# Seven identity matmuls ahead of the gate and up projections of the 31st expert in a two-layer decoder trunk

## The reference, cut to what matters

```python
def hier_moe(h, wg, bg, we, be, w1, w3, w2):
    ...
    def expert_block(args):
        xi, e = args
        hid = jax.nn.silu(xi @ w1[e]) * (xi @ w3[e])
        return hid @ w2[e]
    ...
for l in range(DEPTH):
    ...
    x = x + g1[:, None, :] * y
    h = rms_norm(x) * (1.0 + sc2[:, None, :]) + sh2[:, None, :]
    x = x + g2[:, None, :] * hier_moe(h, ...)
```

## Time and profile before

| | |
|---|---|
| time, median of 3 runs (lowest to highest) | 1340.63 us (1339.63 to 1341.82) |
| span of the profiled execution | 1345.7 us |
| own time of the profiled execution outside its span | none is recorded |
| PE (matmul) busy | 1260.7 us, 94% |
| DMA bytes, mean rate over the span | 493.50 MB, 367 GB/s |
| DMA rate in the slices in which only experts run | 423 to 431 GB/s |
| mean granted clock of TensorE | 0.975 |

### The profile page before, as it was taken

How to read it: one execution, slowest core, us unless ns; L and a number is a source line. 1 busy time by engine, 2 the same in 40 slices (tenths; PEclk the granted TensorE clock), 3 DMA queues, 4 the chain that set the end, 5 groups by cost and what they waited for, 6 DMA issues and landing times.

```text
span 1345.7 us, 15042 instructions
## 1 busy us (share of the span) xinstructions
PE 1260.7 (94%) x6115; PEld 601.4 (45%) x6115; DVE 414.6 (31%) x938; ACT 235.0 (17%) x499; POOL 109.3 (8%) x139
## 2 busy tenths in 40 slices
PE   6999998999999999989898999999999999889988
PEld 3444476433433333434345457743443343333334
DVE  3574864412121121112114983431212211121112
ACT  2223332311111011101110033231101110010101
POOL 2020003000300300210000010000000000000000
PEclk9999999999999999999899998999999999998989
DMA  9992883799999999999999782569999999999993
GB/s 366 407 291 105 329 345 140 289 414 429 428 428 426 429 428 428 429 427 428 428 423 410 284 317 104 211 259 410 431 427 428 427 428 427 428 428 428 428 428 152
DMA packets 51914, 493.50 MB, mean 367 GB/s; under 512 B 4784, under 2 KB 6072, under 8 KB 20992
## 3 DMA queue, kind: packets, MB, share of 16 engines
q1 hardware_dynamic: 49104, 488.85, 87.8%
q10 hardware_dynamic: 1584, 2.69, 0.5%
q0 software_dynamic: 1152, 0.91, 0.5%
HBM read 489.28 MB, written 3.16 MB: 366 GB/s over the span
## 4 chain that ended last, share of the span: by engine, by line
PE 68%; DMA 23%; DVE 5%; issue 1%; ACT 1%; SPq 0%; DVEq 0%; ACTq 0%; PEldq 0%
PE B L872 26%; DMA ring<-in_moe_w 17%; PE B L889 11%; PE A L899 6%; PE A L788 4%; PE B L692 4%; DMA both<-in_moe_w 2%; PE B L705 2%; PE B L635 2%; DMA ring<-in_ada_w 2%; DMA ring<-in_od_w_in 2%; PE A L852 2%; PE B L599 2%; DVE work L1540 1%; PE B L588 1%
## 5 line engine op out<-in xcount | busy, mean ns | idle before, releaser
L872 PE MATMUL B<-ring,work 128*64 128x512 f32 x1488 | 450.2, 616 | 27.2 <-DMA ring<-in_moe_w 19.0
L1534 DVE TENSOR_TENSOR work<-work,B 64x512 f32<-64x512 f32 x64 | 68.3, 1067 | 627.1 <-ACT work L1949 627.1
L872 PEld LDWEIGHTS B<-ring,work 128*64 128x64 f32 x1488 | 140.2, 141 | 230.6 <-issue 230.0
L889 PE MATMUL B<-ring,work 128*64 128x512 f32 x704 | 159.3, 594 | 0.6 <-ACT work L1953 0.6
L1949 ACT ACTIVATE work<-B 64x512 f32<-64x512 f32 x64 | 37.7, 590 | 581.0 <-PE B L872 580.9
L872 PE MATMUL B<-both,work 128*64 128x512 f32 x272 | 124.7, 613 | 5.8 <-DMA ring<-in_moe_w 5.8
L899 PE MATMUL A<-work 128*128 128x256 f32 x512 | 118.1, 384 | 9.3 <-DVE work L1540 9.3
L899 PEld LDWEIGHTS A<-work 128*128 128x128 f32 x512 | 94.6, 190 | 28.8 <-issue 17.2
L2230 POOL COPY work<-work 128x512 f32 x60 | 37.0, 616 | 763.7 <-PE B L872 671.5
L889 PEld LDWEIGHTS B<-ring,work 128*64 128x64 f32 x704 | 50.8, 137 | 94.9 <-issue 94.9
L1540 DVE COPY work<-B 64x512 f32<-64x512 f32 x64 | 43.7, 684 | 121.9 <-PE B L889 121.9
(11 more groups left out here) (312 smaller groups left out, 1129.9 us busy)
## 6 DMA issues: line engine op xcount, KB each, us to landing
ring<-in_moe_w SPq DMA_DIRECT2D x137, 2048.0 KB, 26.9
ring<-in_ada_w SPq DMA_DIRECT2D x24, 2048.0 KB, 18.6
work<-in_moe_w SPq DMA_DIRECT2D x23, 2048.0 KB, 28.4
both<-in_moe_w SPq DMA_DIRECT2D x21, 2048.0 KB, 26.9
early<-in_moe_w SPq DMA_DIRECT2D x11, 2048.0 KB, 29.2
ring<-in_ev_w_in SPq DMA_DIRECT2D x6, 2048.0 KB, 16.1
ring<-in_od_w_in SPq DMA_DIRECT2D x4, 2048.0 KB, 18.1
ring<-in_ev_w_out SPq DMA_DIRECT2D x2, 2048.0 KB, 13.7
```

What stands on the lines that cost most here:

```text
L872: ins = pe.matmul(B5[64 * m:64 * m + 64, :], xs[:, k, :], w[:, k, :], start=(k == 0), stop=(k == KD - 1))
L889: ins = pe.matmul(B7[64 * m:64 * m + 64, :], hidTb[:, k, :], w[:, k, 512 * m:512 * m + 512], start=(k == 0), stop=(k == KF - 1))
L1534: dve.tensor_tensor(hid[64:128, :].rearrange("p (k q) -> p q k", k=KF), silu_a[64:128, :].rearrange("p (q k) -> p q k", k=KF), B5[64:128, ...
```

## The change

In turn q = 30 of each layer, before TensorE waits for the two matrices of the 31st expert, it waits for the copy of the last combine weights out of B4 (the copy that the combine of the same turn needs too) and then issues seven filling matmuls into B4. They read the identity and the first slice of xT, and what they write is read by nobody. Nothing else is changed.

```diff
                         if q > 1:
                             pe.wait_ge(rows_ready, (NE - 2) * l + q - 1)
+                        if q == NE - 2:
+                            pe.wait_ge(main.disp_ev, sbase + G + 2)
+                            keep_running(7, B4)
                         full(n1)
                         full(n3)
                         gate_up(main, xgp[:, :, 0:CH] if q == 0 else xge[:, q % 2], ebase + q, slot8(n1), slot8(n3),
```

## The result

| | before | after |
|---|---|---|
| time, median of 22 runs each | 1341.12 us (1338.25 to 1344.99) | 1345.65 us (1342.06 to 1350.20) |
| ratio, 95% interval | | 1.0027 (1.0019 to 1.0036) |
| span of the profiled execution | 1345.7 us | 1346.2 us |
| MATMUL and LDWEIGHTS instructions | 6115 and 6115 | 6143 and 6143 |

The change makes the kernel slower: by the ratio, which sets runs beside their neighbours, by 3.6 us (2.5 to 4.8); the medians lie 4.5 apart. I had forecast +1.0, no difference that can be told, and a range up to 1344.2. Of the 4.1 between the forecast of 1341.6 and the measured 1345.65, 0.5 is the base (1341.12 over 22 runs, not the 1340.63 of three), 0.9 is the distance between the medians and the ratio, and 2.6 is what the change cost beyond my +1.0.

A forecast was written before the change was run, and what follows sets the result against it. Weight loads were taken to pace later experts, TensorE the end, with waits slowing its clock. 1.7 us lost in layer 0 and 0.7 gained in layer 1 made +1.0 on 1340.63: 1341.6 us, range 1338.6 to 1344.2.

The forecast's parts named there:

- The fill's own cost: On TensorE's queue ahead of the 31st expert: seven calls, 14 instructions, take 3.0 us, 3.2 at most.
- 0.7 gained: Layer 1's 31st expert: with a wait of 2.0, the fill overruns by 1.0 but saves a slow gate-up's 1.7.
- My likelier case: Layer 1: slow 29th gate-up (some 8.78 us), then a 2.0 wait at the 31st, mostly with a slow gate-up behind.
- Layer 0: 31st expert, no wait to fill: TensorE pushed back 3.0, partly absorbed later; 1.7 us lost, bounds 0.4 to 3.0.
- The sum: Whole kernel: 1.7 us lost in layer 0 and 0.7 gained in layer 1, +1.0; the forecast's chance 40%.
- The fill: Step pricing 14 matmuls at 3.0 us on TensorE's queue, the wait ahead free, no other engine reading what they write.
- nothing to save: Rival, layer 1's 31st expert: wait about 2 us or less, clock up anyway, fill only delays; +3.2, 1343.8 us; 22%.
- As profiled: Rival: both layers go as in the profiled execution, 2.15 lost and 2.77 gained; -0.6, 1340.0 us; 28%.
- The fill does not keep the clock up: Rival, 31st expert's gate-up: layer 1 gains nothing, layer 0 loses 2.15; 1342.8 us; 5%.
- Layer 0 absorbed: Rival: sums of squares at line 646 give 1.7 back, layer 1 goes as profiled; -2.3, 1338.3 us; 5%.
- The base: Starting time of the forecast: timed median 1340.63 us; the profiled execution's span, 1345.7, was 5.1 above it.

## Why the prediction was wrong

**The fill's own cost: nearly right.** Seven calls in one place: 3.0 forecast, 3.11 measured.

**Layer 1: right kind, misjudged by a little.** The step "0.7 gained". From the nine waits, the fill of 3.1 overruns by 3.1 less the wait: 0 once, 0.5 to 0.6 five times, 1.9 to 2.3 three times, 1.0 on average; the slow gate-ups it would save come to (2.70 + 1.69 + 1.55 + 1.49 + 1.32) / 9 = 1.0. So about nothing, not 0.7. My likelier case, a slow 29th gate-up and then a wait of 2.0 with another slow one behind it, came in none of the nine: behind the three slow 29ths (8.40 to 8.79) the waits were 1.23, 1.12 and 0.83 and the 31st took 7.09, because the wait behind a fast 29th is mostly 2.5 and not the 3.70 that I subtracted from. The run with layer 1 alone gave +0.5 (-1.5 to +2.5). That the 29th expert decides about the wait at the 31st was right, and filling the 29th showed it.

**Layer 0: the right mechanism, and a size that cannot be told from the measured one.** Forecast +1.7. Nine profiles without the fill have waits at the 31st of 0 three times, about 0.9 four times (0.84 to 1.01), and 2.56 and 2.95 with a slow gate-up behind; overruns average 2.1, less 0.4 saved and 0.1 ahead of the 32nd, that is 1.6 before the slack at the first projection. In the same nine that slack is 0 to 2.4; taken execution by execution it leaves about 1. Alone the fill gave +0.9 (-0.9 to +2.8). The slack varies with the clock in line 646, as I had said for one rival: 0.68 in the first profile, over 2 in two others. In the repeated change line 1146 waited for its DMA again, 1.88, so in that execution the load and not the fill set when layer 1 began.

**The sum: a term was missing.** The step that failed is "The fill": it priced 14 matmuls on TensorE's queue and said that no other engine reads what they write, and stopped there; the sum had no term for a longer program and gave no reason for that. The instructions themselves lengthen TensorE's program, and that put a gap of 2.24 (2.31 in the repeat) into the last transposes, on the path to the output. The stretch to the end became 2.1 longer by it. About 1 for layer 0, 0 for layer 1 and 2.1 make 3.1, against 3.6 (2.5 to 4.8) measured. No rival named it; the one that came closest in size, "nothing to save" at +3.2, had another mechanism, and in layer 1 it is only part of the truth. What stays open is the exact division: five rounds leave each half uncertain by 2 us, and no timed pair isolates the gap clear of noise.

**The rivals.** "As profiled" fell with its draw: one in nine. "The fill does not keep the clock up" is out: behind it every gate-up took 7.09, ahead of layer 0's 29th expert too, where 15 of the 17 profiles without a fill there have a slow one. "Layer 0 absorbed" happens, in some executions.

**The base.** The profile that I argued from was longer than all 22 timed runs. I noted the 5.1 us and drew nothing from it. It had a slow draw in layer 1's mixer (153.8, where nine of 20 took 150.0 to 150.1), which made its span long, and the largest wait at layer 1's 31st expert of nine, which flatters a change that fills waits.

## What to carry to other kernels

Before filling a wait, ask what sets its end. Where loads do, time gained ahead of it only makes the next wait longer, and the fill must be shorter than the shortest wait met over several profiles, not than the one in a single profile. And count the instructions that are added, not only their time: look for "issue" gaps on the engine in places that the change does not touch, above all behind a skipped loop, where both gaps of this case stood, and repeat the change with another number of instructions before believing a difference of 2 us.

## What was not expected of the hardware

- A gap of 2.1 to 2.7 us on TensorE, released by nothing but issue, that came and went with the number of matmul instructions anywhere earlier in the program: with 28 more than before in eight of eight profiles, with 0, 12, 14 and 56 in none of twelve. It kept its place, the 6133rd or 6134th matmul of the program. A second one of 1.07 appeared behind the first layer, in the one program that had 42 more ahead of that point.
- Behind five waits of 2.5 to 2.6 us the same gate-up took 7.09 once and 8.41 to 8.78 four times; the kernel's own time spread over 1337.8 to 1348.7 from one execution to the next.
